# Down projection of a decoder block on one core: two sets of seven products with 512 by 512 weight quarters in place of four pairs of 512 by 256

## The chip, the cores and the metric

The kernel runs on one core of one Trainium2 chip. The metric is the device time of one execution in microseconds (us); lower is better. Three runs of the kernel before give a median of 813.37 us (813.31 to 813.8).

## What is computed

One hybrid decoder block on a sequence of 512 tokens with 1024 channels, all in float32: a gated spatial mixer and a gated linear attention, merged and added to the residual `h`, then the feed-forward part, which the change is about:

```
xn2 = rms_norm(h, norm2_w)
h = h + (silu(xn2 @ w_ffn_gate) * (xn2 @ w_ffn_up)) @ w_ffn_down     # 1024 -> 2816 -> 1024
return rms_norm(h, final_norm_w)
```

`w_ffn_down` has 2816 rows and 1024 columns. The last matrix product, `act @ w_ffn_down`, is called the down projection here.

## The kernel before

**Products.** Every float32 operand is split into a high and a low part of type float32r (`hi` is the rounded value, `lo` the rest), and one product is the sum of three passes: hi by hi, hi by lo, lo by hi. Large matrix products go through a scheme of seven: the activations (rows = tokens) and the weights are each cut into 2 by 2 quarters, and seven products of sums of quarters stand in for eight products of quarters. The seven are named after their weight operand: the plain quarters `A11`, `A12`, `A22` and the sums `S1` to `S4`, which are formed one out of another: S1 = A21 + A22 and S3 = A11 - A21 first, then S2 = S1 - A11, then S4 = A12 - S2. The sums live in PSUM (banks 4 to 7, `chain` and `diff`); the results of the products pass through banks 0 to 3 (and 6, 7 for a wide S2).

**Who does what.** TensorE (PE) runs the seven products of a set in a fixed order. For each, ScalarE (ACT) rounds the weight operand to its high part. The low part is made by GpSimd (POOL) for the plain quarters, and by VectorE (DVE) for the sums; DVE also forms the sums and joins the products' results (they need partial sums of one another). POOL also makes the low parts of the activations `x11`, `x21`, `x22`, `T3`, `T4`, multiplies gate and up (`gated_pair`), and adds finished parts to `h`. SyncE (SP) starts the loads. Each engine has a list written out by hand and works it off in order; semaphores (`op_high`, `s_low`, `plain_low`, `s_formed`, `joined`, `taken`, `product_done`, `h_added` and others) count finished steps, and the waits are for counts of these.

**The down projection before.** The first 2048 of the 2816 rows of `w_ffn_down` go in two chunks of 1024 (`m` = 0 and 1), and each chunk in two halves of 512 output columns: four calls of `down_pair` with p = 18 to 21, each with all seven products. A product has 2 token tiles of 128 by 4 tiles of 128 rows by 256 columns of weights: 24 matmuls 256 wide (`down_product`, L2429 to L2432). Three of the seven (A11, S2, A12) take `wide_down_product` instead: high and low parts lie side by side in one `row` tile, so that 8 matmuls 512 wide (L2440) do hi by hi and hi by lo at once, and 8 matmuls 256 wide (L2444) do lo by hi. The activation tiles stand still in the array and the weights move. The operands of a pair are 128 partitions by 1024 values. The activation sums `T1` to `T4` of a chunk were stored in DRAM earlier and come back through `sum_back`. The weights of a pair come in four loads of 512 KB into `wd[c]`.

**Around it.** Before it stand ten such pairs of the gate and up projections (p = 8 to 17, code line L2195 and next, L2207, L2211); pair 17 (`LAST_FFN`) already prepares the operands of the first set of the down projection. After it, the last 768 rows go in three plain blocks, `down` (`block_N`, L1997 to L1999): 48 matmuls each, 512 wide, for which ACT makes `w_hi` and `ah`, POOL `w_lo` and DVE `al`. Then DVE and ACT normalise and SP stores.

For a pair the list of DVE reads, in the code of `down_pair`: form S2, join, low of S2, form S4, joins, low of S4, form S1 of the next pair, joins, form S3 of the next pair, joins, lows of S1 and S3. `act_t_low_of` (L1812) makes the low parts of T1 and T2; its two inputs both lie in SBUF, as do those of `act_low` (L1780), whereas forms, lows of sums and joins on DVE read at most one of their inputs from SBUF.

Of the kernel before, what the change touches and what calls it, by code (L numbers as in the profile page):

```python
# [30 lines left out]
P = 128  # L31
SEQ = 512
# [32 lines left out]
DOWN_PAIRS = 2 * DOWN_CHUNKS  # L65
# [40 lines left out]
def build(nc, x, x_t, wstream, w_lr, cols, vbias, lnw, lnb, sgub, sgu_wt, w_gk2, ident_d, causal_d, finalw, out):  # L106
    with ExitStack() as ctx:
# [64 lines left out]
        dq = [sb(f"dq{n}", kb, [P, 4, 2, HT]) for n, kb in enumerate((96, 112))]  # L172
# [18 lines left out]
        wd = [sb(f"wd{c}", 16 * c, [P, KD, HALF]) for c in range(2)]  # L191
        row = {n: sb(f"{n}_row", kb, [P, 4, 2 * HT], F32R) for n, kb in SLOT.items()}
        row_hi, row_lo = {n: high_half(t) for n, t in row.items()}, {n: low_half(t) for n, t in row.items()}

        def high_of(name, rows):
            return row_hi[name][:, :, :] if rows else op_hi[name][:, :, :, :]

        def low_of(name, rows):
            return row_lo[name][:, :, :] if rows else op_lo[name][:, :, :, :]

        def weights_of(name, c, rows):
            ks, i = slice(4 * (int(name[2]) - 1), 4 * int(name[2])), int(name[1]) - 1
            return wd[c][:, ks, i * HT:(i + 1) * HT] if rows else wp[c][:, :, ks, i * P:(i + 1) * P]
# [58 lines left out]
        row_chain = acc[:, 4:6, :].rearrange("p a (k n) -> p (a k) n", k=2)  # L262
        row_diff = acc[:, 6:8, :].rearrange("p a (k n) -> p (a k) n", k=2)
# [82 lines left out]
        def loads(p):  # L346
            return MERGE_LOADS[p % 2] + 8 * PAIRS + 32 * ((p - LAST_FFN - 1) // 2 + 1)
# [9 lines left out]
        def _(sp):  # L357
# [78 lines left out]
            def sum_back(p, n):  # L436
                m = (p - LAST_FFN) // 2
                dst, src = sum_raw[n], down_sums[4 * m + n].rearrange("p (k t) -> p k t", k=4)
                sp.wait_ge(t_stored, A_STORED + 64 * (m + 1))
                sp.wait_ge(product_done, 7 * p + (2, 3, 4, 6)[n] - 7)  # L440
                sp.dma_start(dst, src).then_inc(sum_landed[n], 16)

            def down_weights(p):
                c, m, n = p % 2, (p - LAST_FFN - 1) // 2, (p - LAST_FFN - 1) % 2
                for hf, landed in enumerate((k1_landed[c], k2_landed[c])):
                    for j in range(2):
                        k = 4 * hf + 2 * j
                        sp.dma_start(wd[c][:, k:k + 2, :], wstream[W_DOWN + 4 * m + k // 2].rearrange("p (k n) -> p k n", k=2)
                                     [:, :, n * HALF:(n + 1) * HALF]).then_inc(landed, 16)

            for p in range(MERGE_PAIRS + 3, LAST_PAIR + 1):
                ends = p - 2 in (LAST_FFN, LAST_FFN + 2)
                if ends:
                    for n in range(3):
                        sum_back(p - 2, n)
                pair_read((None, p - 2))
                if p <= LAST_FFN:
                    w = W_FFN + 2 * (p - MERGE_PAIRS)
                    pair_weights(wstream[w:w + 2], p % 2)
                else:  # L460
                    down_weights(p)
                if ends:
                    sum_back(p - 2, 3)
            pair_read((None, LAST_PAIR - 1))
            for s in range(2):
                sp.dma_start(raw[s][:, :], wstream[B_DOWN + SKIPPED + s]).then_inc(raw_landed[s], 16)
# [18 lines left out]
        def _(pool):  # L485
# [23 lines left out]
            def plain(name, c, high, rows):  # L509
# [2085 lines left out]
```

## Time and profile before

| | |
|---|---|
| median of 3 runs | 813.37 us |
| the profiled execution | 813.36 us, of which the profiled span is 811.6 us |
| PE busy | 804.5 us (99% of the span), 5096 matmuls |
| DVE, ACT, POOL busy | 568.3, 441.6, 414.0 us (70%, 54%, 51%) |
| pair 17, last of gate and up | 673.9 to 693.9 us on PE |
| down projection in sevens (four pairs) | 693.9 to 773.6 us |
| plain blocks | 773.6 to 806.4 us, end of span 811.6 |

The times of day here and below are us from the start of the span. Matmuls overlap: a matmul 512 wide is listed with 0.39 us, but the next starts 0.23 us after it, so what a stretch costs is read from starts, not from the sum of durations.

### The profile page before, as it was taken

What the parts mean: (1) busy time and instruction counts of PE and PEld (TensorE: products, weight loads), DVE (VectorE), ACT (ScalarE), POOL (GpSimd) and SP (SyncE); (2) the same over time, 40 slices, a digit from 0 to 9 for tenths busy, and PEclk for the clock granted to TensorE, in tenths of its full rate; (3) what the DMA queues carried; (4) which work ended last, traced back from release to release, by engine and by line L of the source; (5) the groups of instructions that cost most, each with busy time, mean ns of one, the idle gap of its engine ahead of it and who ended that gap; (6) DMA issues with size and microseconds to landing.
All of it is one profiled execution on the core that took longest, in us unless ns stands there. A gap on an engine that the chain in (4) does not pass through costs nothing.

```text
span 811.6 us, 12616 instructions
## 1 busy us (share of the span) xinstructions
PE 804.5 (99%) x5096; PEld 728.8 (90%) x5096; DVE 568.3 (70%) x612; ACT 441.6 (54%) x501; POOL 414.0 (51%) x146
## 2 busy tenths in 40 slices
PE   9999999999999999999999999999999999999997
PEld 7888888888888899999998899999999999999985
DVE  5377377364774967898984278777778888878836
ACT  5522446756656555867442575545455446665624
POOL 4445424424224533477955443544444445878880
PEclk9999999999999999999999999999999999999999
DMA  7972422121132363333135303433334445536022
GB/s 293 265 278 104 160 100 96 61 103 52 52 105 104 104 208 105 105 105 104 73 135 212 104 1 105 126 111 108 108 108 159 161 162 190 184 125 222 1 78 103
DMA packets 29868, 103.09 MB, mean 127 GB/s; under 512 B 2816, under 2 KB 7296, under 8 KB 25856
## 3 DMA queue, kind: packets, MB, share of 16 engines
q1 hardware_dynamic: 24592, 87.07, 31.5%
q10 hardware_dynamic: 5232, 15.40, 5.9%
q8 instruction: 31, 0.51, 0.3%
q14 instruction: 13, 0.11, 0.0%
HBM read 94.08 MB, written 8.39 MB: 126 GB/s over the span
## 4 chain that ended last, share of the span: by engine, by line
PE 99%; DMA 0%; ACT 0%; issue 0%; SPq 0%; DVE 0%; ACTq 0%
PE acc L2195 10%; PE acc L2197 9%; PE acc L2198 9%; PE acc L2207 9%; PE acc L1980 7%; PE acc L1982 7%; PE acc L1981 6%; PE acc L1999 6%; PE acc L1997 6%; PE acc L1998 6%; PE acc L2211 5%; PE acc L2440 3%; PE acc L2026 3%; PE acc L2429 2%; PE acc L2432 2%; PE acc L2431 2%
## 5 line engine op out<-in xcount | busy, mean ns | idle before, releaser
L490 POOL TENSOR_TENSOR w_lo<-raw,w_hi 128x2048 fp32r<-128x2048 f32 x26 | 122.8, 4721 | 163.1 <-ACT w_hi L685 162.9
L511 POOL TENSOR_TENSOR A_lo<-wp,A_hi 128x1024 fp32r<-128x1024 f32 x51 | 126.2, 2475 | 142.6 <-ACT A_hi L860 135.2
L875 ACT ACTIVATE S_hi<-acc 128x1024 fp32r<-128x1024 f32 x68 | 68.1, 1024 | 89.9 <-PE acc L2198 34.4
L1484 DVE TENSOR_TENSOR S_lo<-acc,S_hi 128x1024 fp32r<-128x1024 f32 x68 | 81.7, 1219 | 13.1 <-ACT S_hi L875 13.0
L1980 PE MATMUL acc<-xt,w_hi 128*128 128x512 f32 x224 | 88.0, 393 | 0.0
L1982 PE MATMUL acc<-xt,w_lo 128*128 128x512 f32 x224 | 87.2, 389 | 0.0
L1981 PE MATMUL acc<-xt,w_hi 128*128 128x512 f32 x224 | 87.2, 389 | 0.0
L685 ACT ACTIVATE w_hi<-raw 128x2048 fp32r<-128x2048 f32 x26 | 49.6, 1911 | 66.2 <-PE acc L1999 53.6
L860 ACT ACTIVATE A_hi<-wp 128x1024 fp32r<-128x1024 f32 x51 | 53.8, 1055 | 17.4 <-PE acc L2198 17.4
L1982 PEld LDWEIGHTS acc<-xt,w_lo 128*128 128x128 f32 x224 | 42.1, 188 | 8.8
L1980 PEld LDWEIGHTS acc<-xt,w_hi 128*128 128x128 f32 x224 | 42.1, 188 | 8.7
L1981 PEld LDWEIGHTS acc<-xt,w_hi 128*128 128x128 f32 x224 | 42.1, 188 | 8.5
L2195 PE MATMUL acc<-tb,S_hi 128*128 128x256 f32 x168 | 47.7, 284 | 0.0
L2198 PE MATMUL acc<-tb,S_lo 128*128 128x256 f32 x168 | 47.5, 283 | 0.0
L2197 PE MATMUL acc<-tb,S_hi 128*128 128x256 f32 x168 | 47.5, 283 | 0.0
L2195 PE MATMUL acc<-mt,S_hi 128*128 128x256 f32 x136 | 38.7, 285 | 0.0
L2197 PE MATMUL acc<-mt,S_hi 128*128 128x256 f32 x136 | 38.5, 283 | 0.0
L2198 PE MATMUL acc<-mt,S_lo 128*128 128x256 f32 x136 | 38.5, 283 | 0.0
L1997 PE MATMUL acc<-w_hi,xw_hi 128*128 128x512 f32 x96 | 37.3, 389 | 0.0
L1998 PE MATMUL acc<-w_lo,xw_hi 128*128 128x512 f32 x96 | 37.3, 389 | 0.0
L1999 PE MATMUL acc<-w_hi,xw_lo 128*128 128x512 f32 x96 | 37.3, 389 | 0.0
L2207 PE MATMUL acc<-ft,A_hi 128*128 128x512 f32 x144 | 36.1, 392 | 0.0
(376 smaller groups left out, 2522.6 us busy)
## 6 DMA issues: line engine op xcount, KB each, us to landing
wp<-wstream SPq DMA_DIRECT2D x34, 1024.0 KB, 7.8
raw<-wstream SPq DMA_DIRECT2D x26, 1024.0 KB, 4.9
wd<-wstream SPq DMA_DIRECT2D x16, 512.0 KB, 6.5
down_sums<-act_sum ACTq DMA_DIRECT2D x8, 512.0 KB, 3.5
sum_raw<-down_sums SPq DMA_DIRECT2D x8, 512.0 KB, 3.7
xn_in<-x ACTq DMA_DIRECT2D x4, 512.0 KB, 7.4
turned_sums<-tx ACTq DMA_DIRECT2D x4, 512.0 KB, 3.8
raw_out<-wstream SPq DMA_DIRECT2D x2, 1024.0 KB, 5.9
```

What stands on the lines that cost most here:

```text
L490: pool.tensor_tensor(w_lo[s][:, :], raw[s][:, :], w_hi[s][:, :], ALU.subtract).then_inc(lo_ready, 1)
L511: pool.tensor_tensor(low_of(name, rows), weights_of(name, c, rows), high_of(name, rows), ALU.subtract).then_inc(plain_low, 1)
L1980: pe.matmul(dst, wh[:, k, cs], rh[:, k, ts], start=(k == 0), stop=False)
L1981: pe.matmul(dst, wh[:, k, cs], rl[:, k, ts], start=False, stop=False)
L1982: last = pe.matmul(dst, wl[:, k, cs], rh[:, k, ts], start=False, stop=(k == KD - 1))
L1997: pe.matmul(dst, lh[:, k, ts], wh[:, k, cs], start=(first and k == 0), stop=False, skip_group_check=resumed)
L1998: pe.matmul(dst, lh[:, k, ts], wl[:, k, cs], start=False, stop=False, skip_group_check=resumed)
L1999: mm = pe.matmul(dst, ll[:, k, ts], wh[:, k, cs], start=False, stop=((last or pause) and k == 1), skip_group_check=resumed)
L2195: pe.matmul(dst, wh[:, g, k, :], x[0][:, k, :], start=(start and g == 0 and k == 0), stop=False, skip_group_check=True)
L2197: pe.matmul(dst, wh[:, g, k, :], x[1][:, k, :], start=False, stop=False, skip_group_check=True)
L2198: mm = pe.matmul(dst, wl[:, g, k, :], x[0][:, k, :], start=False, stop=(k == 3), skip_group_check=True)
L2207: pe.matmul(by_bank(bank[banks[g]]), wh[:, g, k, :], both[:, k, :, :], start=(start and k == 0), stop=False, skip_group_check=True)
```

## The change

The four pairs become two sets (`down_half(m)`, m = 0 and 1), one for each chunk of 1024 rows, over all 1024 output columns. A quarter of the weights is now 512 rows by 512 columns (128 partitions by 2048 values), loaded into a tile of its own (`wd["A11"]` and so on, two loads of 512 KB each), and each product is 24 matmuls of 512 columns; the `row` tiles with high and low side by side are gone. Operands take turns in three slots (`slot_hi`, `slot_lo`), a product's result takes two banks, by turns 0, 1 and 2, 3, and one chain in banks 4 to 7 holds S1, S2, S4; S3 is formed in SBUF, over A21. The order of the products is now A11, S1, A12, S2, S3, A22, S4. Results that are final go straight onto `h` on DVE (`onto_h`); two partial sums (`first_part`, `part_sum`) are added to `h` by POOL (`add`). The lists of all five engines between pair 17 and the plain blocks are new, and the low part of the first plain block moves from POOL to DVE. The weights' columns, the number of columns moved and the scheme are the same.

```diff
+ORDER = ("A11", "S1", "A12", "S2", "S3", "A22", "S4")
+PLAIN_ORDER, SUMS_FORMED, SUMS_LOW = ("A11", "A12", "A22"), ("S3", "S1", "S2", "S4"), ("S1", "S2", "S3", "S4")
+JOINS, ADDS = ("h22", "h12", "h11", "u1", "u2", "h21", "h12_done"), ("h12", "h21", "h22")
...
+        slot_hi = [sb(f"slot_hi{n}", kb, [P, 4, HALF], F32R) for n, kb in enumerate((181, 40, 197))]
+        slot_lo = [sb(f"slot_lo{n}", kb, [P, 4, HALF], F32R) for n, kb in enumerate((32, 189, 96))]
+
+        def slot_of(m, name):
+            return (7 * m + ORDER.index(name)) % 3
...
+        def product_banks(m, name):
+            b = 2 * ((m + ORDER.index(name)) % 2)
+            return acc[:, b:b + 2, :]
...
+            def pair(p, c, n, nn, first=False, last=False, q=None):
...
+                if last:
+                    down_plain_high(0, "A11", 7 * LAST_FFN - 6)
+                    act_t(0, 0)
+                    half_copy(0, 5 * LAST_FFN - 4)
...
+            def down_halves():
+                pair_silu((None, LAST_FFN))
+                down_plain_high(0, "A12", 7 * LAST_FFN)
+                act_x(7 * LAST_FFN, 0, f22, slice(4, 8), slice(HT, SEQ))
+                act_t(0, 3)
+                take_first(0)
+                down_sum_high(0, "S2", product_of(0, "A11"))
...
             def pair(p, c, nn, first=False, q=None):
...
+                if last:
                     act_t_low_of(0, 0)
-                form_s3(1 - c, rows)
-                if q == PAIRS:
+                    down_s3(0)
                     act_t_low_of(0, 1)
+                else:
+                    form_s3(1 - c)
                 if not first:
                     join_c11(p)
                 if q is not None and q != PAIRS:
                     act_sums(q)
+                if last:
+                    down_s1(0)
                 join_c21(p)
...
+            def down_halves():
+                join_c12((None, LAST_FFN))
+                v.wait_ge(product_done, 7 * LAST_FFN - 1)
+                down_sum_low(0, "S1")
+                down_s2(0)
+                v.wait_ge(h_landed, 16)
+                down_sum_low(0, "S2")
+                down_s4(0)
+                onto_h(0, "S1", 1, 1)
+                onto_h(0, "S1", 0, 1)
+                down_sum_low(0, "S3")
+                onto_h(0, "A12", 0, 0)
+                act_t_low_of(1, 0)
+                onto_first(0)
+                down_sum_low(0, "S4")
+                onto_part(0)
+                down_s3(1)
+                down_s1(1)
+                act_t_low_of(1, 1)
+                v.wait_ge(h_added, added_of(0, "h21"))
+                onto_h(0, "A22", 1, 0)
+                down_sum_low(1, "S1")
...
-            def down_product(name, x, b, start):
-
-                wh, wl = row_hi[name], row_lo[name]
+            def down_product(m, name, x, start=True):
+
+                wh, wl = slot_hi[slot_of(m, name)], slot_lo[slot_of(m, name)]
+                dst = product_banks(m, name)
                 for t in range(2):
-                    dst = bank[b][:, t * HT:(t + 1) * HT]
                     ts = slice(t * P, (t + 1) * P)
                     for k in range(4):
-                        pe.matmul(dst, x[0][:, k, ts], wh[:, k, :], start=(start and t == 0 and k == 0), stop=False,
+                        pe.matmul(dst[:, t, :], x[0][:, k, ts], wh[:, k, :], start=(start and k == 0), stop=False,
                                   skip_group_check=True)
...
+                pe.wait_ge(plain_low, plain_of(m, "A11"))
+                pe.wait_ge(refill_low, renewed + 1)
+                if m == 0:
+                    pe.wait_ge(taken, 2 * LAST_FFN)
+                else:
+                    pe.wait_ge(joined, join_of(m - 1, "h21"))
+                down_product(m, "A11", x11)
...
+                pe.wait_ge(s_low, low_sum_of(m, "S2"))
+                pe.wait_ge(t_low, A_LOW + 2 * m + 2)
+                pe.wait_ge(joined, join_of(m, "h12"))
+                down_product(m, "S2", t2)
```

Two places in the order of the instructions. The first is DVE's list at the hand-over from pair 17 to the down projection. `u3`, `cq` are joins of pair 17, `tb0`, `tb1` receive the low parts of T1 and T2, `acc` is PSUM. Before:

```order
L1466 TENSOR_TENSOR acc<-acc,wd0_137 128x1024 [waits k2_landed0,a21_copied,s_low]
L1758 TENSOR_TENSOR u3_78<-acc,u2_77 128x512 [waits joined,product_done]
L1761 TENSOR_TENSOR cq_73<-acc,u3_78 128x512 [waits joined,pair_ready]
L1812 TENSOR_TENSOR tb0_117<-sum_raw0_104,tb0_117 128x4x256 [waits t_high]
L1470 TENSOR_TENSOR acc<-wd0_137,acc 128x1024
L1812 TENSOR_TENSOR tb1_118<-sum_raw1_105,tb1_118 128x4x256 [waits t_high]
L1745 TENSOR_TENSOR cq_73<-acc,cq_73 128x512 [waits low_taken]
L1761 TENSOR_TENSOR cq_73<-acc,u2_77 128x512 [waits product_done]
L1484 TENSOR_TENSOR S1_row_140<-acc,S1_row_140 128x4x256 [waits op_high]
```

And with the change, on to the joins of the first results of the first set:

```order
L1811 TENSOR_TENSOR u3_78<-acc,u2_77 128x512 [waits joined,product_done,s_low]
L1814 TENSOR_TENSOR cq_73<-acc,u3_78 128x512 [waits joined,pair_ready]
L1865 TENSOR_TENSOR tb0_117<-sum_raw0_104,tb0_117 128x4x256 [waits t_high]
L1870 TENSOR_TENSOR wd_A21_138<-wd_A11_137,acc 128x2048 [waits k1_landed0,a21_copied]
L1865 TENSOR_TENSOR tb1_118<-sum_raw1_105,tb1_118 128x4x256 [waits t_high]
L1798 TENSOR_TENSOR cq_73<-acc,cq_73 128x512 [waits low_taken]
L1874 TENSOR_TENSOR acc<-acc,wd_A22_139 128x2048 [waits k1_landed1]
L1814 TENSOR_TENSOR cq_73<-acc,u2_77 128x512 [waits product_done] x2
L1889 TENSOR_TENSOR slot_lo1_145<-acc,slot_hi1_142 128x2048 [waits op_high,product_done]
L1878 TENSOR_TENSOR acc<-acc,wd_A11_137 128x2048 [waits s_low]
L1889 TENSOR_TENSOR slot_lo0_144<-acc,slot_hi0_141 128x2048 [waits op_high,h_landed]
L1883 TENSOR_TENSOR acc<-wd_A12_140,acc 128x2048 [waits k2_landed1,s_low]
```

S1 was formed ahead of u3 and is now formed behind both T lows, form S3 and the join of `cq`; behind the last row shown come the two `h<-acc,h` that empty the banks of product S1.

The second place is POOL's list at the same hand-over. Before:

```order
L511 TENSOR_TENSOR A22_lo_132<-wp1_122,A22_hi_125 128x1024 [waits op_high]
L511 TENSOR_TENSOR A11_row_139<-wd0_137,A11_row_139 128x4x256 [waits op_high]
L578 TENSOR_TENSOR tb2_119<-sum_raw2_106,tb2_119 128x4x256 [waits t_high]
L511 TENSOR_TENSOR A12_row_145<-wd0_137,A12_row_145 128x4x256 [waits op_high]
L573 TENSOR_TENSOR ft_120<-act_91,ft_120 128x4x256 [waits refill_high]
L567 TENSOR_TENSOR act_91<-silp_74,cq_73 128x1024 [waits silp_ready,t_stored]
```

And with the change:

```order
L566 TENSOR_TENSOR A22_lo_132<-wp1_122,A22_hi_125 128x1024 [waits op_high]
L638 TENSOR_TENSOR slot_lo0_144<-wd_A11_137,slot_hi0_141 128x2048 [waits op_high,product_done]
L633 TENSOR_TENSOR tb2_119<-sum_raw2_106,tb2_119 128x4x256 [waits t_high]
L628 TENSOR_TENSOR ft_120<-act_91,ft_120 128x4x256 [waits refill_high]
L622 TENSOR_TENSOR act_91<-silp_74,cq_73 128x1024 [waits silp_ready,t_stored]
L638 TENSOR_TENSOR slot_lo2_146<-wd_A12_140,slot_hi2_143 128x2048 [waits op_high,pair_ready]
```

The low part of A11 is one instruction of 2048 values per partition where it was one of 1024, and that of A12 now stands behind x21's low part and the product of gate and up.

## Rows read from the trace of the kernel before

**Rows 1.** The profile page: busy time of each engine, and the granted clock of TensorE.

```profile
PE 804.5 (99%) x5096; PEld 728.8 (90%) x5096; DVE 568.3 (70%) x612; ACT 441.6 (54%) x501; POOL 414.0 (51%) x146
PEclk9999999999999999999999999999999999999999
```

**Rows 2.** Waits of PE in the whole span: total us, times, longest.

```profile
PE acc L2016 <- DVE ones_dv L1242: 1.2, 1, 1.2
PE acc L2026 <- ACT xw_hi L709: 0.7, 1, 0.7
```

**Rows 3.** Timeline of PE in the down projection: start, us, what, count.

```profile
693.73 0.28 PE L2198 MATMUL acc<-ft,S_lo 128*128 128x256 f32 x1
693.85 0.86 PE L2440 MATMUL acc<-A_row,ft 128*128 128x512 f32 x3
...
745.14 2.00 PE L2440 MATMUL acc<-A_row,ft 128*128 128x512 f32 x8
746.98 1.11 PE L2444 MATMUL acc<-A_row,ft 128*128 128x256 f32 x8
747.93 0.28 PE L2429 MATMUL acc<-A_row,ft 128*128 128x256 f32 x1
748.05 0.28 PE L2431 MATMUL acc<-A_row,ft 128*128 128x256 f32 x1
```

**Rows 4.** The same timeline over the plain blocks, first and last of 144 matmuls.

```profile
773.60 0.40 PE L1997 MATMUL acc<-w_hi,ah 128*128 128x512 f32 x1
...
806.04 0.39 PE L1999 MATMUL acc<-w_hi,al 128*128 128x512 f32 x1
```

**Rows 5.** Groups of instructions from 560 us on: mean ns of one behind the comma.

```profile
L1484 DVE TENSOR_TENSOR S_row<-acc,S_row 128x1024 fp32r<-128x1024 f32 x16 | 19.3, 1217 | 1.9 <-ACT S_row L875 1.9
L490 POOL TENSOR_TENSOR w_lo<-raw,w_hi 128x2048 fp32r<-128x2048 f32 x3 | 14.4, 4801 | 3.1 <-ACT w_hi L685 3.1
L573 POOL TENSOR_TENSOR ft<-act,ft 128x1024 fp32r<-128x1024 f32 x6 | 14.5, 2413 | 2.1 <-ACT ft L1146 2.1
L1860 DVE TENSOR_TENSOR dq<-acc,u 128x512 f32<-128x512 f32 x12 | 8.3, 688 | 3.6 <-PE acc L2432 3.1
L685 ACT ACTIVATE w_hi<-raw 128x2048 fp32r<-128x2048 f32 x3 | 5.6, 1907 | 16.1 <-PE acc L1999 16.1
L1152 ACT ACTIVATE tb<-sum_raw 128x1024 fp32r<-128x1024 f32 x6 | 6.3, 1048 | 0.0
```

**Rows 6.** Busy time by window: window, us, PE (x) PEld (x) DVE (x) ACT (x) POOL (x), clock.

```profile
680.00:720.00 40.00, 40.00 (x291) 37.94 (x290) 32.29 (x35) 25.86 (x29) 31.30 (x14) 1.00 0.48 158
720.00:760.00 40.00, 40.00 (x290) 37.90 (x289) 31.99 (x34) 23.82 (x27) 34.55 (x15) 1.00 0.46 158
```

**Rows 7.** Timeline of POOL around three instructions of DVE.

```profile
686.23 2.41 POOL L511 TENSOR_TENSOR A_row<-wd,A_row 128x1024 fp32r<-128x1024 f32 x1 [0.45 <-ACT A_row L860]
...
766.30 5.17 POOL L490 TENSOR_TENSOR w_lo<-raw,w_hi 128x2048 fp32r<-128x2048 f32 x1 [0.41 <-ACT w_hi L685]
```

**Rows 8.** Timeline of DVE: three instructions with both inputs in SBUF.

```profile
687.80 1.92 DVE L1812 TENSOR_TENSOR tb<-sum_raw,tb 128x1024 fp32r<-128x1024 f32 x1
...
690.78 1.21 DVE L1812 TENSOR_TENSOR tb<-sum_raw,tb 128x1024 fp32r<-128x1024 f32 x1
...
768.29 4.26 DVE L1780 TENSOR_TENSOR al<-act,ah 128x1024 fp32r<-128x1024 f32 x1
```

**Rows 9.** Timeline of DVE and ACT in pair 17, the steps that stay as they are.

```profile
682.62 1.03 ACT L875 ACTIVATE S_hi<-acc 128x1024 fp32r<-128x1024 f32 x1 [1.73 <-PE acc L2211]
...
687.19 0.69 DVE L1761 TENSOR_TENSOR cq<-acc,u 128x512 f32<-128x512 f32 x1
```

**Rows 10.** Timeline at the start: PE takes up work that ACT releases.

```profile
5.19 0.72 ACT L709 ACTIVATE xw_hi<-xw,par 128x512 fp32r<-128x512 f32 x1 [1.47 <-DMA par<-cols]
5.97 1.20 PE L2026 MATMUL acc<-w_hi,xw_hi 128*128 128x512 f32 x4 [0.69 <-ACT xw_hi L709]
```

**Rows 11.** DMA issues from 640 us on: KB each, median us to landing.

```profile
wd<-wstream SPq DMA_DIRECT2D x16, 512.0 KB, 6.5
sum_raw<-down_sums SPq DMA_DIRECT2D x8, 512.0 KB, 3.7
```

More of the change, by code:

```diff
@@ L64 @@
 DOWN_CHUNKS = 2
-DOWN_PAIRS = 2 * DOWN_CHUNKS
 K_PLAIN = KD * DOWN_CHUNKS
@@ L451, in _ @@
[L451 to L455, printed above, removed]
-                pair_read((None, p - 2))
[L457 to L463, printed above, removed]
@@ new lines, in _ @@
+            for p in range(MERGE_PAIRS + 3, LAST_FFN + 1):
+                pair_read((None, p - 2))
+                w = W_FFN + 2 * (p - MERGE_PAIRS)
+                pair_weights(wstream[w:w + 2], p % 2)
+            pair_read((None, LAST_FFN - 1))
+            down_weights(0, "A21")
+            down_weights(0, "A11")
+            sum_back(0, 0)
+            sum_back(0, 1)
+            pair_read((None, LAST_FFN))
+            down_weights(0, "A22")
+            sum_back(0, 2)
+            down_weights(0, "A12")
@@ new lines, in _, with read @@
+            sum_back(0, 3)
+            def read(m, formed, plain=None):
+                sp.wait_ge(s_formed, formed_of(m, formed))
+                if plain is not None:
+                    sp.wait_ge(plain_low, plain_of(m, plain))
+            read(0, "S2", "A11")
+            down_weights(1, "A11")
+            sum_back(1, 0)
+            read(0, "S4", "A12")
+            down_weights(1, "A12")
+            sp.wait_ge(s_low, low_sum_of(0, "S3"))
+            down_weights(1, "A21")
+            sum_back(1, 1)
@@ L467, in _ @@
+            read(0, "S1", "A22")
+            down_weights(1, "A22")
+            sum_back(1, 2)
+            sum_back(1, 3)
+            read(1, "S2", "A11")
+            sp.dma_start(raw[0][:, :], wstream[B_DOWN + SKIPPED]).then_inc(raw_landed[0], 16)
+            sp.wait_ge(s_low, low_sum_of(1, "S3"))
+            sp.dma_start(raw[1][:, :], wstream[B_DOWN + SKIPPED + 1]).then_inc(raw_landed[1], 16)
             sp.wait_ge(hi_ready, N_BLKS - 2)
@@ L1829, in pair @@
                 v.wait_ge(s_low, at(p, 4))
-                form_s1(1 - c, nn, at(p, 1, 1), rows)
+                if not last:
+                    form_s1(1 - c, nn, at(p, 1, 1))
                 if not first:
@@ L2498, in down @@
+            for m in range(DOWN_CHUNKS):
+                down_half(m)
             def down(m, s, first=False, last=False, pause=False):
```

568 lines of the change are left out of this document (262 added, 306 removed).

## The prediction

> **What bounds the kernel now.** I read the page first: PE is busy for 99% of the span, at the higher of its two clock levels (2.4 GHz) in all 40 slices [rows 1]. Then the waits: in the whole span PE waits 1.9 us, all of it before 6 us [rows 2]. So nothing but PE's own stream sets the end until 806.4 us, and each us that the stream loses or gains between 694 and 774 us reaches the end: the plain blocks behind it run from start to finish without a gap [rows 4], and the last 5 us hang on the last matmul. Then the timeline, for what a matmul costs there. The reader should go by starts. The down projection in sevens starts at 693.85 and the plain blocks at 773.60: 79.75 us [rows 3, 4]. A matmul 256 wide starts 0.12 us after the one before it; eight 512 wide take 1.84 us, 0.230 each, and the eight 256 wide behind them 0.95 us [rows 3]. In the plain blocks 143 starts take 32.44 us, 0.2269 each [rows 4].
>
> **The stream itself.** Before, a pair has 24 matmuls of 512 and 24 + 96 of 256: four pairs make 96 and 480, so 96 x 0.230 + 480 x 0.120 = 79.7 us, as seen. After, 14 products x 24 = 336 matmuls of 512. Their form, weight rows contiguous and 512 wide, activations standing, is that of the plain blocks [rows 4], so 336 x 0.2269 = 76.2 us. The columns are the same (172,032); what goes is the fixed part of 240 matmuls, (79.75 - 76.2)/240 = 15 ns each. **Gain 3.5 us.**
>
> The Trainium skill speaks against that gain: "TensorE: Matmul & The Clock Gate", section "Back-to-back issue gap", puts the fixed part at 2.5 ns per matmul whatever its width. By it 240 matmuls are worth an estimated 0.6 us, and the sum below would end at about 817.3. The trace does not agree for this stream (0.120 and 0.2269 us leave about 13 ns), so I take the rows.
>
> **What must keep up.** A product now lasts 24 x 0.2269 = 5.45 us and a set 38.1 us. Operands are twice as long, three slots are in use, two sets of banks take turns, so an operand and a pair of banks must be ready one or two products later. Durations for 2048 values: ACT 1.9 us (L685) [rows 5]; POOL 4.6 to 4.8 (L490) [rows 5], I take 4.7; DVE 2.3, from 1.22 for 1024 and 0.69 for 512 [rows 5]. By amount it fits: DVE has, per set, 4 forms and 4 lows of 2.3, 7 joins of 1.2 and 2 T lows, some 30 us; POOL 3 lows of 4.7 and about 9 pieces of 2.4, some 35 us; ACT less (before, DVE was busy 32, POOL 31 to 35, ACT 24 to 26 of 40 us [rows 6]). It is the order that costs.
>
> **A wait that the trace shows, and that grows.** A DVE instruction whose two inputs both lie in SBUF does not run beside an instruction of POOL. T1's low takes 1.92 us at 687.80 while POOL works until 688.64 (688.64 + 1.1 = 689.72); with POOL idle it takes 1.21. `al` takes 4.26 us at 768.29, POOL's `w_lo` ends at 771.47, and 771.47 + 1.1 is its end [rows 7, 8]. So it waits for POOL's instruction to end, and POOL's instructions are now 4.7 us long.
>
> **The list, step by step.** Pair 17 on PE stays. A restart of PE costs some 0.15 us beyond the release: at 5.97 us it starts right after ACT, but its first four starts take longer than three steps of 0.227 [rows 10].
> - *A11, set 0.* ACT ends S4's high at 683.6 [rows 9], A11's high at 685.5. POOL makes its low until 690.2. DVE is through with `u3` and `cq` at 686.9 (before at 687.9 [rows 9], with form S1 ahead), then T1's low is held until 690.2 and ends at 691.3. Form S3 693.5, T2's low 694.6, the join of `cq` 695.2, for whose banks PE waits. It was due at 693.85 and starts at 695.4: **1.5 us.**
> - *S1.* Its form stood ahead of all that; now it follows: 697.4, high on ACT 699.4, low 701.7. Due 700.9: **1.1 us.** A22's load is no cause: issued at 685.6 it lands by 692.1 [rows 11].
> - *A12.* POOL does the product of gate and up first, which waits for the last joins and the Silu (700.3): 702.8, then A12's low 707.5. Due 707.4: **0.2 us.**
> - *S2.* It needs the banks of S1, whose result DVE adds onto `h` in two instructions placed behind S2's low and form S4: form S2 704.1; on ACT behind A12, x22, T4 and `first_part`, S2's high 706.9; low 709.2, form S4 711.5, the two adds 713.8. Due 713.1: **0.9 us.**
> - *S3, A22, S4 of set 0.* By the same list joins and lows are in time by 1.7 to 3.9 us: **0**, the cover being two products of 5.45 us.
> - *A11, set 1.* Its banks wait for the join of A22, which stands behind forms S3 and S1 and T2's low of set 1, and that is held by POOL's low of A11 (729.4 to 734.1): 735.2, join 736.3. Due 735.7: **0.75 us.**
> - *The rest of set 1.* A12's low on POOL is ready 0.7 us ahead, the banks for S2 0.9 us: **0**, thinly.
> - *The plain blocks.* w_lo of the first, now on DVE, is made in product S4's 5.45 us (2.3 us, plus at most 1.5 of POOL's last add); that of the second starts on POOL after S4 and has 10.9 us. **0.** SP's list has the same 16 and 8 loads; the sums that stood before the weights no longer do. **0.**
>
> Stalls 4.5 us, against 3.5: the profiled execution's 813.36 + 1.0 = 814.3 us (span 812.6), and since it is 0.01 from the median of the runs, the same for the median. The bounds of the stalls: with the shortest durations (POOL 4.6, no delay between engines) 4.1; with 0.05 to 0.1 us more at each hand-over 5.3: 813.9 to 815.1.
>
> **Rivals.**
> - *The stream runs on, the stalls are hidden (faster).* For it: the stall of A11 begins with a DVE instruction that misses POOL by 1.3 us; without that hold S1 and the rest fall in time, and the full 3.5 us stand: 809.8; with half of the stalls 812. Against it: three rows show the hold, and the list leaves no other order. 0.2.
> - *POOL falls behind in set 1 (slower).* Place: POOL's chain low of A11, add, T3, x21, low of A12, which two holds of DVE (T2, low of S3, now 2.3 us) lengthen; margin 0.7 us, from which on each 0.1 us is paid by PE in full, first at A12 and then at S2, whose margins are of one size. A low of 2048 slowed as `w_lo` at 766.30 was (5.17 for 4.7 [rows 7]), twice, and a hold more of 1.1 each give 2 to 3 us: 816.5 to 817.5. For it: 35 us of work in 38. 0.22.
> - *The narrow matmul's fixed part does not go* (the page's rule, as a mechanism here: the 0.2269 of the plain blocks belongs to their operands, and the new stream runs at 0.235, the 512 wide rows' 0.230 and a little): 336 x 0.235 = 79.0, gain 0.8: 817.0. Against it: both rows with 512 are under 0.231 [rows 3, 4]. 0.03. By the page's own figure above it would be 817.3.
>
> **How the numbers follow.** A measurement of this kernel can tell 0.2%, 1.6 us, from no change: faster is below 811.7, slower above 815.0. The forecast has 0.55, of which 0.45 within and 0.1 above 815.0; the first rival 0.2 faster; the other two 0.25 slower. So faster 0.2, same 0.45, slower 0.35. The likeliest case alone holds 813.5 to 815.3; the range for all reaches to 811.0 and 817.2, leaving out the full gain and the worst of the second rival.
>
> **What would show it.** Right: in the changed profile the starts of the down products 0.227 us apart; PE with waits, which it had not, at the first matmul of A11, S1 and S2 of set 0 and A11 of set 1, released by DVE; T1's low about 4.4 us long and ending 1.1 us after POOL's low of A11. Wrong: no PE waits after 694 us (first rival), waits on POOL's lows in set 1 (second), starts 0.23 or more apart (third). PE's total wait above 6 us or below 2 would say that the list of steps is not what decides.

## The result, and the profile after the change

| | before | after |
|---|---|---|
| median | 813.43 us of 22 runs (813.1 to 816.05) | 815.39 us of 22 runs (814.49 to 816.92) |
| the profiled execution (span) | 813.36 (811.6) | 814.49 (812.8) |
| starts of the sevens and of the plain blocks | 693.85 and 773.60 | 695.40 and 774.75 |

The ratio of after to before is 1.0023, 95% interval 1.0017 to 1.003: 2.0 us slower by the medians, 1.1 us by the two profiled executions. By the prediction's own bound (0.2%, 815.0 us) that counts as slower, to which it had given 0.35, and not as no change, to which it had given 0.45. Half of the runs of after lie within 0.9 us of its lowest and the rest up to 2.4 us above it. The profiled one is the shortest of its 22, and that turns out to matter.

The page of the profile after, against [rows 1]:

```profile
span 812.8 us, 12041 instructions
PE 802.9 (99%) x4856; PEld 716.5 (88%) x4856; DVE 568.7 (70%) x579; ACT 437.5 (54%) x479; POOL 402.5 (50%) x137
```

240 matmuls fewer (4856 for 5096), 1.6 us less of busy PE, and yet a longer span. PE's waits, against [rows 2]:

```profile
PE acc L2501 <- DVE cq L1798: 1.5, 1, 1.5
PE acc L2088 <- DVE ones_dv L1301: 1.2, 1, 1.2
PE acc L2501 <- DVE h L1893: 1.2, 2, 0.7
PE acc L2501 <- DVE slot_lo L1889: 0.7, 1, 0.7
```

L2501 is the first matmul of a product. Its four waits are new, and the timeline has their places (first matmul of A11 and its next, then S1, S2, A11 of set 1, and the plain blocks, against [rows 3, 4]):

```profile
695.40 0.47 PE L2501 MATMUL acc<-slot_hi,ft 128*128 128x512 f32 x1 [1.52 <-DVE cq L1798]
695.71 0.39 PE L2503 MATMUL acc<-slot_lo,ft 128*128 128x512 f32 x1
...
701.83 0.50 PE L2501 MATMUL acc<-slot_hi,tb 128*128 128x512 f32 x1 [0.74 <-DVE slot_lo L1889]
...
713.83 0.47 PE L2501 MATMUL acc<-slot_hi,tb 128*128 128x512 f32 x1 [0.46 <-DVE h L1893]
...
736.58 0.47 PE L2501 MATMUL acc<-slot_hi,ft 128*128 128x512 f32 x1 [0.71 <-DVE h L1893]
...
774.75 0.39 PE L2069 MATMUL acc<-w_hi,ah 128*128 128x512 f32 x1
```

From 736.58 on the seven products of set 1 run without a wait: 7 x 24 matmuls until 774.75 are 38.17 us, 0.227 each. The wait in brackets counts from the modelled end of the matmul before, 0.39 us long. The delay of a start is larger: 701.83 - 695.40 is 6.43 us for a product of 5.45, so S1 is 1.0 late and not 0.74. A start can also be late without a wait in the list: A12 starts at 707.63, 5.80 after S1, right behind the end of POOL's low part of A12 at 707.58.

DVE's timeline at the hand-over, where the first wait comes from, against [rows 8]:

```profile
686.83 4.49 DVE L1865 TENSOR_TENSOR tb<-sum_raw,tb 128x1024 fp32r<-128x1024 f32 x1
691.24 2.27 DVE L1870 TENSOR_TENSOR wd_A<-wd_A,acc 128x2048 f32<-128x2048 f32 x1
693.44 1.21 DVE L1865 TENSOR_TENSOR tb<-sum_raw,tb 128x1024 fp32r<-128x1024 f32 x1
694.57 0.68 DVE L1798 TENSOR_TENSOR cq<-acc,cq 128x512 f32<-128x512 f32 x1
```

And POOL's instruction beside the first of these, against [rows 7]:

```profile
685.60 4.64 POOL L638 TENSOR_TENSOR slot_lo<-wd_A,slot_hi 128x2048 fp32r<-128x2048 f32 x1
```

T1's low (the first row of DVE) takes 4.49 us in place of 1.21 and ends at 691.32, 1.08 us behind the end of POOL's instruction at 690.24.

### The profile page after: what moved, and what is told of

It is laid out like the page before. It is cut to its first block, busy times and chain, and to the rows that moved or that the text cites. A ratio compares the mean times of both kernels' runs of the same rounds, so it can differ in the third digit from the quotient of the medians.

```text
span 812.8 us, 12041 instructions
## 1 busy us (share of the span) xinstructions
PE 802.9 (99%) x4856; PEld 716.5 (88%) x4856; DVE 568.7 (70%) x579; ACT 437.5 (54%) x479; POOL 402.5 (50%) x137
## 4 chain that ended last, share of the span: by engine, by line
PE 93%; DVE 4%; ACT 1%; issue 1%; DVEq 0%; ACTq 0%
PE acc L2267 9%; PE acc L2269 9%; PE acc L2270 9%; PE acc L2279 9%; PE acc L2052 7%; PE acc L2054 6%; PE acc L2053 6%; PE acc L2071 6%; PE acc L2069 6%; PE acc L2070 6%; PE acc L2283 4%; PE acc L2098 3%; DVE tb L1865 2%; PE acc L2501 2%; PE acc L2504 2%; PE acc L2503 2%
## 5 line engine op out<-in xcount | busy, mean ns | idle before, releaser
L545 POOL TENSOR_TENSOR w_lo<-raw,w_hi 128x2048 fp32r<-128x2048 f32 x25 | 117.6, 4703 | 171.8 <-ACT w_hi L738 168.0
L926 ACT ACTIVATE S_hi<-acc 128x1024 fp32r<-128x1024 f32 x68 | 68.1, 1024 | 89.8 <-PE acc L2270 34.4
```

The source lines that it names most:

```text
L545: pool.tensor_tensor(w_lo[s][:, :], raw[s][:, :], w_hi[s][:, :], ALU.subtract).then_inc(lo_ready, 1)
```

## Experiments

Each kernel is compared with the kernel before, run beside it on the same chip: the median of before is 813.36 us for experiments 1 to 4, 813.64 for 5, 6, 7 and 9, and 813.63 for 8, 10 and 11.

**1. The change once more, unedited.**

> The changed kernel once more, unedited, as the yardstick of this call. The profiled execution of the change ended at 814.49 us with four waits of PE in the down projection (1.5, 0.74, 0.46 and 0.7 us), the median of its 22 runs is 815.39. Theory A (order of the instructions alone makes the stalls): the same four waits again within 0.1 us each, the start of the plain blocks at 774.7 to 774.9, and what a longer execution has more lies outside the down projection. Theory C (the returns of the sums T1 to T4 from DRAM, for which ACT waits up to 3 us ahead of the high parts of A22 and A11, come at times that vary): another execution shows other waits of ACT on sum_raw and a PE wait or more that changes by 0.5 to 2 us with them; the median is 0.9 us above the first profile for that reason.

Measured: 815.95 us (6 runs, 814.73 to 817.13), ratio 1.003 (1.0018 to 1.0041). The profiled execution took 816.5 us, and its waits are another set:

```profile
PE acc L2501 <- DVE h L1893: 2.1, 1, 2.1
PE acc L2501 <- POOL slot_lo L638: 1.6, 1, 1.6
...
PE acc L2501 <- DVE cq L1798: 1.1, 1, 1.1
...
PE acc L2501 <- DVE slot_lo L1889: 0.7, 1, 0.7
```

A11 of set 1 waits 2.1 us, and A12 of set 0, which had no wait, 1.6 us for POOL. POOL's timeline has the origin 30 us earlier. In the profile of the change:

```profile
675.19 2.40 POOL L566 TENSOR_TENSOR A_lo<-wp,A_hi 128x1024 fp32r<-128x1024 f32 x1 [6.68 <-DMA down_sums<-act_sum]
```

and in this one:

```profile
678.24 2.42 POOL L566 TENSOR_TENSOR A_lo<-wp,A_hi 128x1024 fp32r<-128x1024 f32 x1 [9.51 <-DMA down_sums<-act_sum]
```

POOL waits for the store of the activation sums ahead of its whole list of pair 17. ACT issued the store at 671.9 and 672.1, so it landed after 3.3 and 6.1 us. From there the lateness runs on: pair 17's low part of A22 ends at 685.6 or 687.7; SyncE, which waits for it, issues A22's load and behind it T3's return. T3's return as ACT waits for it, in ACT's timeline of the change:

```profile
693.66 1.06 ACT L1206 ACTIVATE tb<-sum_raw 128x1024 fp32r<-128x1024 f32 x1 [3.01 <-DMA sum_raw<-down_sums]
```

and in that of this run:

```profile
695.99 1.06 ACT L1206 ACTIVATE tb<-sum_raw 128x1024 fp32r<-128x1024 f32 x1 [5.11 <-DMA sum_raw<-down_sums]
```

In the trace of before the same instruction stands at 690.68 and waits for nothing. POOL makes T3's low part after it, then x21's, the product of gate and up, and A12's low part. In set 1 it is T2's return: ACT waits for it 2.96 us until 724.49 in the profile of the change, 4.69 us until 726.82 here, with the copy of A21 and A11's high part queued behind. So the same program has other waits in another execution, and they go with the returns, as theory C says; that the returns are their cause is shown by experiments 5 to 7.

The wait at A11 of set 0 has changed its place too. POOL was later here, so T1's low got in ahead of its low part of A11, and T2's low was held in its stead, in DVE's timeline:

```profile
690.96 3.46 DVE L1865 TENSOR_TENSOR tb<-sum_raw,tb 128x1024 fp32r<-128x1024 f32 x1
```

POOL's instruction ends at 693.33 and this one 1.09 us later.

**2. POOL's long instruction in two halves.**

```diff
-pool.tensor_tensor(slot_lo[n][:, :, :], wd[name][:, :, :], slot_hi[n][:, :, :], ALU.subtract).then_inc(plain_low, 1)
+pool.tensor_tensor(slot_lo[n][:, 0:2, :], wd[name][:, 0:2, :], slot_hi[n][:, 0:2, :], ALU.subtract)
+pool.tensor_tensor(slot_lo[n][:, 2:4, :], wd[name][:, 2:4, :], slot_hi[n][:, 2:4, :], ALU.subtract).then_inc(plain_low, 1)
```

(for A11 of set 0 alone)

> POOL's low part of A11 of set 0 as two instructions of 1024 values in place of one of 2048, nothing else. Theory A (DVE's instruction with two SBUF inputs waits for the end of POOL's whole instruction): T1's low fits behind the first half, takes about 2.3 us in place of 4.49 and ends near 689.2; join cq, S1's form and low come some 2 us earlier; the waits of PE at A11 and S1 of set 0 shrink from 1.5 and 0.74 to under 0.3 each, that at S2 (two joins behind form S4) stays or grows to about 0.7, A11 of set 1 keeps 0.7: start of the plain blocks 772.3 to 772.9, time 2.0 to 2.4 us below the changed kernel, near 813.2 as a median. Rival B (the stall at A11 comes from the amount of work at the hand-over, and the hold is hidden or only moves to another DVE instruction): within 0.5 us of the changed kernel, 815.0 to 815.4, with T1's low still over 4 us or a later low held in its place.

Measured: 816.35 us (5 runs, 814.97 to 817.38), ratio 1.0038 (1.0025 to 1.0051). The median lies above both expectations; the profiled execution, 815.26 us, is one of the two short ones of the five. T1's low shrinks to 2.67 us, and A11 starts at 693.86 with no wait. But the gain is gone 14 us later, at A12, and A11 of set 1 waits too, both behind the late returns:

```profile
700.39 0.50 PE L2505 MATMUL acc<-slot_hi,tb 128*128 128x512 f32 x1 [0.90 <-DVE slot_lo L1893]
708.09 0.50 PE L2505 MATMUL acc<-slot_hi,ft 128*128 128x512 f32 x1 [1.96 <-POOL slot_lo L642]
...
737.34 0.47 PE L2505 MATMUL acc<-slot_hi,ft 128*128 128x512 f32 x1 [1.76 <-DVE h L1897]
```

The hold is real and was worth nothing here, because the chain through T3's return bound at the next place. Why the median is no better than 816.35 this profile does not show.

**3. The two additions of S1's result ahead of form S4.**

```diff
+onto_h(0, "S1", 1, 1)
+onto_h(0, "S1", 0, 1)
 down_s4(0)
-onto_h(0, "S1", 1, 1)
-onto_h(0, "S1", 0, 1)
```

> The two additions of product S1's result onto h moved ahead of form S4 in DVE's list of set 0, nothing else. It removes the cause of the wait at S2 (0.46 us in the profile): the banks are free 2.3 us earlier. Theory A says each stall removed alone shows again at the next place that binds: form S4, S3's low and S4's low come 2.3 us later in the list, T1's low of set 1 and with it the list at A11 of set 1 too, so its wait grows from 0.7 to about 1.4: the time stays within 0.3 us of the changed kernel (815.2 to 815.6). Rival B (the four stalls add up independently, each is worth what it shows): 0.4 to 0.5 us less, 814.9, with A11 of set 1 still at 0.7.

Measured: 815.96 us (6 runs, 815.16 to 818.49), ratio 1.0035 (1.0023 to 1.0047): no difference from the unedited kernel, 0.4 above the range of theory A. PE did not wait at S2; it waited 1.40 at A12 and 1.48 at A11 of set 1. This does not show what the edit does for S2: in experiment 1, without the edit, PE did not wait there either, because A12 was late before it.

**4. Both, and T2's low of set 1 ahead of form S3 of set 1.** Besides the edits of 2 and 3:

```diff
 onto_part(0)
+act_t_low_of(1, 1)
 down_s3(1)
 down_s1(1)
-act_t_low_of(1, 1)
```

> Three edits together: POOL's low part of A11 of set 0 in two instructions; the two additions of S1's result ahead of form S4; T2's low of set 1 ahead of form S3 of set 1, so that it does not wait behind POOL's low of A11 of set 1. Theory A: each of the prediction's four stalls loses its cause; PE's waits in the down projection sum to 0 to 0.5 us, the plain blocks start at 771.1 to 771.8, which is the full 3.5 us of the stream less than half a us: 3.0 to 3.6 us below the changed kernel, near 812.1, and 0.998 of the kernel before (0.9975 to 0.9985). Rival B (stalls turn up behind other instructions because DVE and POOL are short of time in all): 813.5 to 815. Theory C (spread by the returns of T): the first profile may be this good, but the median lies 0.5 to 1 us above it and the runs spread by 2 us as those of the change do.

Measured: 815.1 us (11 runs, 812.61 to 817.32), ratio 1.0018 (1.0009 to 1.0028). Expected were 812.1. The edits take away the cause that the prediction named for each of four stalls, yet only those at A11 of either set are gone for certain (S2 does not wait, but A12 was late before it, as in 3). S1 waits longer than in the change, and its cause is T3's return again: ACT takes S1's high part behind T3's, which waited 4.84 us for its landing:

```profile
701.28 0.50 PE L2505 MATMUL acc<-slot_hi,tb 128*128 128x512 f32 x1 [1.42 <-DVE slot_lo L1893]
...
696.00 1.06 ACT L1210 ACTIVATE tb<-sum_raw 128x1024 fp32r<-128x1024 f32 x1 [4.84 <-DMA sum_raw<-down_sums]
```

A12 waits 1.96 us for POOL, as in 2, and something new stands in PE's timeline behind that wait:

```profile
709.77 0.39 PE L2505 MATMUL acc<-slot_hi,ft 128*128 128x512 f32 x1
710.00 0.52 PE L2507 MATMUL acc<-slot_lo,ft 128*128 128x512 f32 x1
710.32 0.63 PE L2508 MATMUL acc<-slot_hi,ft 128*128 128x512 f32 x1
710.74 0.63 PE L2505 MATMUL acc<-slot_hi,ft 128*128 128x512 f32 x1
...
713.30 0.50 PE L2505 MATMUL acc<-slot_hi,ft 128*128 128x512 f32 x1
713.64 0.39 PE L2507 MATMUL acc<-slot_lo,ft 128*128 128x512 f32 x1
```

The starts are 0.427 us apart for 3.3 us. The table of windows (window, us, PE busy, clock, DMA share, GB/s) gives the granted clock as the last column but two:

```profile
710.00:711.00 1.00, 1.00 (x4) 0.56 1.00 354
711.00:712.00 1.00, 1.00 (x3) 0.50 0.12 41
712.00:713.00 1.00, 1.00 (x4) 0.50 0.00 0
713.00:714.00 1.00, 1.00 (x5) 0.73 0.00 0
```

0.50 is the lower level, 1.2 GHz. A12 takes 7.19 us from its start to that of S2, in place of 5.57 (A12 of experiment 1, restarted after a wait too): 1.6 us. So a wait of PE can cost more than itself: in this profile the clock comes on top of S1's 1.42 and A12's 1.96. The mean clocks of the eleven runs part them cleanly: the four at 0.999 or 1.0 take 812.61 to 814.51 us, the seven at 0.996 or 0.997 take 815.09 to 817.32.

**5. T3's return issued first, in SyncE's list.**

```diff
+sum_back(0, 2)
 pair_read((None, LAST_FFN))
 down_weights(0, "A22")
-sum_back(0, 2)
```

> Only SyncE's list changes: the return of sum T3 of set 0 is issued before the wait for pair 17's weights and before A22's two loads, as in the kernel before. Theory C (the order of the returns): T3's high part on ACT no longer waits for its landing (it waited 3.0 us in the profile of the change and 5.1 in the second profile) and stands at 690 to 691 in place of 693.7 to 696; POOL's T3, x21 and product of gate and up are through by 702.9 (bound by the Silu), so PE's wait on POOL's low part at A12 of set 0 (1.64 us in the second profile) is gone, and a wait of 0.5 us at S2 stands in its place. The returns of set 1 still vary, so A11 of set 1 keeps 0.7 to 2.1 us. Median 0.7 to 1.2 us below the unedited change of the last call (815.95), that is 814.8 to 815.3. Theory A alone (order on DVE and POOL, the landing hidden): no difference, 815.95 within 0.3.

Measured: 815.66 us (7 runs, 815.09 to 816.28), ratio 1.0028 (1.0016 to 1.0039). T3's high is at 690.42 with no wait and A12 has no wait, as expected; the median fell by 0.3 and not by 0.7 to 1.2 (0.6 when each is taken against the kernel before beside it). The trace has a reason on the other side: POOL now makes T3's low at 691.54, while DVE wants T2's low (two inputs in SBUF):

```profile
693.47 1.55 DVE L1865 TENSOR_TENSOR tb<-sum_raw,tb 128x1024 fp32r<-128x1024 f32 x1
```

1.55 us in place of 1.21, and T1's low was 4.66 in place of 4.49; together that is the 0.5 by which A11's wait grew, to 2.03 us. The late return had kept POOL out of the way of DVE's T2 low.

**6. POOL's wait for the store moved to the one instruction that needs it.**

```diff
 def pair(p, c, first=False):
...
+    if p[0] is None and p[1] - 1 >= MERGE_PAIRS + 8:
+        pool.wait_ge(t_stored, A_STORED + 64 * (p[1] - 1 - MERGE_PAIRS - 7))
     if not first:
         gated_pair((p[0], p[1] - 1))
...
-    if p - 1 >= MERGE_PAIRS + 8:
-        pool.wait_ge(t_stored, A_STORED + 64 * (p - 1 - MERGE_PAIRS - 7))
     pair((None, p), p % 2)
```

> Only POOL's wait for the stores of the activation sums moves: from ahead of pair 17's list to ahead of its product of gate and up, behind two low parts that do not need it. In the profile of the change the store landed 3.3 us after its issue (POOL starts at 675.19), in the second 6.1 us after (678.24), and that made pair 17's last low part end at 685.6 against 687.7, and with it SyncE's issue of A22's load and of T3's return 2.1 us later. Theory C with the store as first cause: POOL's low part of A11 starts at 685.6 in every execution, T3's return is issued near 687.0 and lands near 693.6, A12 of set 0 does not wait or under 0.3 us; median 0.7 to 1.2 us below the unedited change, 814.8 to 815.3. If the landing of the returns themselves varies (4 to 7 us) and not the store, the median stays near 815.9.

Measured: 814.91 us (11 runs, 814.5 to 815.23), ratio 1.0017 (1.0008 to 1.0026). The spread of the runs is 0.7 us where the change's is 2.4, all at the lower end of its range. POOL no longer waits for a DMA there, in its timeline:

```profile
674.08 2.40 POOL L566 TENSOR_TENSOR A_lo<-wp,A_hi 128x1024 fp32r<-128x1024 f32 x1 [5.49 <-ACT A_hi L913]
```

So with the wait for that store off the path the upper half of the change's runs is gone: the varying landing of one store, with what follows from it, had most of the part in their spread. The waits of PE are those of the first profile (1.55, 0.73, 0.47, 0.98 us, the last 0.3 longer).

**7. All returns off the path.** 5 and 6 together, and in set 1, on ACT and on DVE:

```diff
-act_t(1, 1)
 half_copy(1)
 down_plain_high(1, "A11", product_of(0, "S3"))
+act_t(1, 1)
...
-act_t_low_of(1, 1)
 v.wait_ge(h_added, added_of(0, "h21"))
 onto_h(0, "A22", 1, 0)
+act_t_low_of(1, 1)
```

> The two edits above together, and in set 1 ACT takes T2's high part behind the copy of A21 and A11's high part (it waited 3.0 and 4.7 us for that return in the two profiles, with those two queued behind it), and DVE makes T2's low behind the addition of A22's result. Theory C: nothing of the down projection hangs on a DRAM round trip any more. Waits of PE: A11 1.5, S1 0.7, S2 0.5 as in the profile of the change, A11 of set 1 under 0.5 (the held low of T2 no longer stands ahead of it); plain blocks from 773.9 to 774.4; median 814.0 to 814.5, and a spread of the runs of under 1.5 us where the unedited change has 2.4. Rival: the spread is of another origin (clock, the first 30 us); then it stays and the median is above 815.

Measured: 815.16 us (11 runs, 814.51 to 817.21), ratio 1.0022 (1.0013 to 1.0031). Expected were 814.0 to 814.5. A11 of set 1 no longer waits at all, S2 0.23, A12 of set 1 0.28. But A11 of set 0 waits 2.03 as in 5:

```profile
696.41 0.76 PE L2501 MATMUL acc<-slot_hi,ft 128*128 128x512 f32 x1 [2.03 <-DVE cq L1798]
```

and behind it the clock falls, in the table of windows:

```profile
696.00:697.00 1.00, 0.59 (x2) 0.71 0.97 348
697.00:698.00 1.00, 1.00 (x4) 0.50 0.37 129
698.00:699.00 1.00, 1.00 (x4) 0.50 0.00 0
699.00:700.00 1.00, 1.00 (x4) 0.58 0.00 0
```

A11 takes 7.16 us there, 1.6 more than after a wait without that, but S1, which would have been 1.0 late, now is not: part of the price was due anyway. Eight of the 11 runs have a mean clock of 0.996 or 0.997, as the profiled one, and take 814.99 to 817.21 us; the three above take 814.51 to 814.92, still just over what was expected.

**8. The same kernel with POOL's low of A11 in two** (the edit of 2).

> The kernel of the run 'returns' (815.16) with POOL's low part of A11 of set 0 in two instructions, and nothing else: the same single edit as in 'split', now with the landings of the sums T1 to T4 off the path. Theory A (T1's low is held behind POOL's whole instruction, 4.5 us, and that is the stall of A11 and S1): A11's wait of 2.0 us goes, S1 waits for its low part about 1 us (its form waits for A22's landing at 694), net gain 1.3 to 1.8 us; the wait at S2 for the two additions behind form S4 shows with 0.3 to 1.0: median 813.2 to 814.2. If the gain of 'all_edits' (2.5 us below 'returns') came from the additions instead, this one is at 814.8 to 815.2.

Measured: 812.57 us (12 runs, 811.79 to 813.96), ratio 0.9989 (0.998 to 0.9997). The edit that was worth nothing in 2 is worth 2.6 us here, more than the 1.3 to 1.8 expected. T1's low is no longer held, in DVE's timeline, and A11 starts with no wait, in PE's:

```profile
687.18 2.29 DVE L1869 TENSOR_TENSOR tb<-sum_raw,tb 128x1024 fp32r<-128x1024 f32 x1
...
694.07 0.40 PE L2505 MATMUL acc<-slot_hi,ft 128*128 128x512 f32 x1
```

That is 694.07 in place of 696.41, and no clock falls; the plain blocks start at 772.70 in place of 775.35. S1 waits 0.55, S2 0.44 and A12 of set 1 0.22.

**9. With the additions of 3 on top** (that diff on the kernel of 8).

> The kernel of the run before with POOL's low part of A11 of set 0 in two instructions and the additions of S1's result ahead of form S4. Theories A and C together: all four stalls have lost their cause, none is left that a landing decides; A12's low part on POOL is then bounded by the Silu of pair 17 and the product of gate and up (through at 701.3 to 702.8, low part until 706 to 707.5), so PE waits at A12 or before it for 1 to 2 us of the 2.3 that A11 and S1 lose, and nowhere else more than 0.3: plain blocks from 771.4 to 772.8, median 811.5 to 813.0, the first version below the kernel before (813.36). If it is above 813.4, the amount of work on POOL and DVE at the hand-over, and not its order, is what costs.

Measured: 812.66 us (11 runs, 811.71 to 813.67), ratio 0.999 (0.9981 to 0.9999). No difference from 8: S2's wait of 0.44 is gone, A12 of set 1 waits 0.92 for POOL in place of 0.22, and S1 1.12, because form S1 waits 0.71 for A22's landing at 694.2 (DVE's timeline):

```profile
694.22 2.30 DVE L1878 TENSOR_TENSOR acc<-acc,wd_A 128x2048 f32<-128x2048 f32 x1 [0.71 <-DMA wd_A<-wstream]
```

**10. Two more steps of POOL moved**, on the kernel of 9, with A22's load first in SyncE's list again (5 undone) and PE's counts for x21 and T3 of set 1 to match:

```diff
+if last:
+    a22_low(c, at(p, 7, 6 - 7))
...
     gated_pair((p[0], p[1] - 1))
-a22_low(c, at(p, 7, 6 - 7))
+if not last:
+    a22_low(c, at(p, 7, 6 - 7))
...
-act_t_low(2, 1, 7)
 act_x(5, 1, f21, slice(4, 8), slice(0, HT))
 down_low(1, "A12")
+act_t_low(2, 1, 7)
```

> The kernel of 'all_edits' (812.66) with two more steps of POOL moved: pair 17's low part of A22 ahead of its product of gate and up, and with it SyncE's load of the first set's A22 2.3 us earlier, with T3's return behind the load again; and in set 1 T3's low part behind A12's low part. In 'all_edits' form S1 waited 0.7 us for A22's landing (694.2) and PE waited 1.1 us at S1 for what follows, and 0.9 us for POOL's low part at A12 of set 1. Theory A: A22 lands near 692, S1's wait shrinks to about 0.4; A12 of set 1 no longer waits; nothing else moves: plain blocks at 771.8 to 772.4, median 811.2 to 812.0, ratio to the kernel before 0.997 to 0.998. Rival: landing times of weights and sums move against each other (the DMA engines share the load) and what A22 gains T3 loses; then 812.2 to 812.9.

Measured: 811.08 us (6 runs, 810.39 to 812.52), ratio 0.997 (0.9958 to 0.9982): faster than the kernel before by 0.3%, and 0.1 us below the range expected. The edits came together, so what each is worth is not known; the waits at S1 (1.12) and at A12 of set 1 (0.92) are down to 0.33 and nothing. The fourteen products take 77.2 us, 694.00 to 771.17, and PE's waits name one that is left in them:

```profile
PE acc L2509 <- DVE slot_lo L1897: 0.3, 1, 0.3
```

**11. The matmuls of 9 as two of 256 each.**

```diff
-for k in range(4):
-    pe.matmul(dst[:, t, :], x[0][:, k, ts], wh[:, k, :], ...)
+for c in (slice(0, HT), slice(HT, HALF)):
+  for k in range(4):
+    pe.matmul(dst[:, t, c], x[0][:, k, ts], wh[:, k, c], ...)
```

(and the other two matmuls alike)

> The kernel of 'all_edits' with each matmul of the seven products of both sets, 512 columns wide, as two of 256 with their own load of the activation tile: 672 matmuls in place of 336 over the same columns and operands. By the rows of before a matmul of 256 starts 0.120 us after the one before it, one of 512 0.2269, so 2 x 0.120 - 0.2269 = 0.013 us of fixed part for each of the 336 more: starts 0.120 apart, a product 5.76 us long in place of 5.45, the 14 products +4.4 us, of which what PE waits for in 'all_edits' (about 2 us) is partly hidden by it: 815.0 to 817.2, about 2.5 to 4.4 us above 'all_edits'. By the Trainium skill, TensorE: Matmul & The Clock Gate, section Back-to-back issue gap, the fixed part is 2.5 ns, and the kernel would be an estimated 0.8 us longer at most, 812.7 to 813.5, with starts about 0.115 apart.

Measured: 815.03 us (10 runs, 814.31 to 815.41), ratio 1.0015 (1.0006 to 1.0024), at the lower edge of the forecast by rows and 1.5 us above the one by the Trainium skill's figure. PE's timeline within a product:

```profile
704.25 0.28 PE L2506 MATMUL acc<-slot_hi,tb 128*128 128x256 f32 x1
704.37 0.28 PE L2508 MATMUL acc<-slot_lo,tb 128*128 128x256 f32 x1
704.49 0.28 PE L2509 MATMUL acc<-slot_hi,tb 128*128 128x256 f32 x1
```

Starts 0.120 apart; from 694.26 to the plain blocks at 775.25 it is 81.0 us, and PE's waits show none among the products. Against the kernel of 10, where almost none is left either, the sevens are 3.8 us longer and the medians differ by 3.95, for 336 matmuls more: 11 to 12 ns each. In the products that run undisturbed in both it is 13 ns: nine of them take 51.84 us here (717.65 to 769.49), 5.76 each, and ten in the kernel of 10 take 54.40 (711.33 to 765.73), 5.44 each. Against its own base (9) it is 2.4 us, because the longer products cover the waits of that kernel. The Trainium skill's 2.5 ns (TensorE: Matmul & The Clock Gate, section Back-to-back issue gap) would be an estimated 0.8 us; the measurements decide for the rows. That section gives its 2.5 ns for the gap of an isolated matmul and says that in a stream of weight loads and matmuls both set the spacing, so the figure spoke less against the gain than the prediction took it to.

## Why the prediction was right, and where it was not

The forecast was 814.3 us, with the likeliest case from 813.5 to 815.3. The median, 815.39, lies just beyond that and within the whole range; the ratio of 1.0023 is just over the 0.2% that the prediction named as what can be told. Against the profiled execution, for which the sum was made, the forecast is 0.2 us off, against the median 1.1 us. The mechanism is right; that the sum meets the profiled execution so closely is luck in part, since that one is the shortest of 22, and the second profile, 816.5 us with other waits, would have been missed by 2.2.

- **The stream, gain 3.5 us: right.** 0.227 us a matmul, and 77.2 us for all fourteen products once the waits are gone (experiment 10), against 76.2 plus 0.3 of wait and some restarts. Experiment 11 gives the fixed part back: 11 to 12 ns a matmul over the whole kernel and 13 in the undisturbed products, where the sum had 15 from the whole stretch and 13 from the steps.
- **A11 of set 0, 1.5 us: right in size and cause.** Start at 695.40, foretold 695.4; T1's low 4.49 us, ending 1.08 behind POOL. Experiments 2 and 8 take the hold away and the wait with it.
- **S1, 1.1 us: right** (1.0 by the starts). **A12, 0.2 us**: 707.63, foretold 707.6. **S2, 0.9 us**: 713.83, foretold 714.0. **A11 of set 1, 0.75 us**: 736.58 against 736.45; DVE's T2 low of set 1 is held as foretold, 3.18 us until 735.29. The plain blocks: 774.75 against 774.6.
- **SP's list at 0: the step that failed.** "SP's list has the same 16 and 8 loads; the sums that stood before the weights no longer do. **0.**" Moved behind a wait that hangs on POOL, and POOL's list behind a store whose landing took from 3.3 to 6.1 us, T3's return stood on the path, and T2's of set 1 on ACT's list. In the first profile that happened to cost nothing. In the second the plain blocks started 2.0 us later, at 776.76. Against the median all that the sum lacks is 0.9 us (815.39 against 814.49), and most of it is this term: with the wait for the store out of the way (experiment 6) the median is 814.91, 0.5 lower, or 0.7 with both taken against the kernel before beside them. The rest was not measured alone.
- **One execution behind every row.** The landings of [rows 11] were taken as fixed (3.7 us for a return, where the changed profiles have 4.9 and 5.6), and no term of the range stood for their change from run to run.
- **The rival "POOL falls behind in set 1"**: not in set 1 and not by held instructions in the changed kernel. Its place was A12 of set 0. In set 1 POOL's low of A12 bound only when the rest was repaired (0.3 us in experiment 7, 0.2 in 8, 0.9 in 9).
- **"The stalls are hidden"**: refuted by the trace; each stall is where it was put. **The narrow matmul's fixed part**: it does go, by the 0.227 us between starts and by experiment 11.

Taking the stalls away one by one (experiments 2 to 4) did not show their size: several chains end within 2 us of one another, and the next one takes over. Only when the returns were off the path did the same edit show its 2.6 us, of which 2.3 are seen at A11's start. The clock of most runs of 7 has a small part in that: the three of its runs whose mean clock is 0.998 or more lie 1.9 to 2.4 us above the median of 8.

**Left open.** When a wait of PE brings the clock down: one of 2.03 us at A11 did in the profile of 7 and did not in that of 5; one of 1.96 us at A12 did in 4 and did not in 2; and 2.1 us at A11 of set 1 did not in 1. The four of the change's 22 runs whose mean clock is 0.997 or less take 815.77 to 816.71 us, all above its median, so the clock has a part in its spread too; its share was not measured alone.

## What to carry to other kernels

Halving the number of matmuls by making them twice as wide was worth 12 to 13 ns here for each matmul saved; but every operand is twice as long, and the time that one engine holds another up grows with the longest single instruction, which can be cut in two. When a transfer moves behind another wait in a queue, price it as a chain (who issues it, behind which wait, landing time at its longest), because a round trip through DRAM is the term that varies from run to run. And where an edit that should help does nothing, look in its trace for the wait that took over before giving up the reason: remove that, then try again.

## What the runs showed of the hardware that was not expected

- **DVE and POOL hold each other, both ways.** In experiment 1 T1's low started at 687.05, before POOL's low of A11, and ended at 688.84; POOL's instruction took 5.62 us, in place of 4.64, and ended 4.49 after it (POOL's timeline):

```profile
687.71 5.62 POOL L638 TENSOR_TENSOR slot_lo<-wd_A,slot_hi 128x2048 fp32r<-128x2048 f32 x1
```

  Who comes first makes the other wait for a whole instruction. The Trainium skill (GPSIMD Engine Reference, section 1. Specifications) names contention of POOL with VectorE's instructions that have two inputs in SBUF; the trace agrees and adds the size: a hold until the other's end and about the full duration behind it (1.08 of 1.21 us for DVE, 4.49 of 4.64 for POOL).
- **TensorE's clock can fall to 1.2 GHz behind a wait of some 2 us in a stream that is otherwise full**, for over 3 us, and makes that product 1.6 us longer (experiments 4 and 7).
- **One store of 512 KB landed between 3.3 and 6.1 us after its issue** in two executions of one program (4.0 in the profile of the kernel before).
